# A fused two-block layer on one core: the down-projection weights of each routed expert loaded through GpSimd's software queue

## The chip, the core and the metric
One Trainium2 chip, one core. The engines are TensorE (PE; its weight loads are shown apart as PEld), VectorE (DVE), ScalarE (ACT), GpSimd (POOL) and SyncE (SP). A transfer issued by an engine is carried out by the core's 16 DMA engines; the profile calls SP's queue q1, ACT's q10 and GpSimd's software queue q0. The metric is the device time of one execution in microseconds (us).

## The reference
Two blocks run in series on 512 tokens of width 1024, all in float32. The first mixes by convolutions and spatial gating and looks up single experts (PEER). The second has attention, memory attention and, at its end, the stage of this change, a mixture of 32 experts with four experts for each token:

```python
logits = (hf @ w_router + b_router).astype(jnp.float32)
top_val, top_idx = lax.top_k(logits, TOP_K)          # TOP_K = 4
gates = jax.nn.softmax(top_val, axis=-1)
...
def expert_block(args):
    e, tok, g = args
    xb = hf[tok]
    gu = xb @ w1[e] + b1[e]
    gate = jnp.minimum(gu[:, :D_FF], SWIGLU_LIMIT)
    up = jnp.clip(gu[:, D_FF:], -SWIGLU_LIMIT, SWIGLU_LIMIT)
    act = (up + 1.0) * gate * jax.nn.sigmoid(SWIGLU_ALPHA * gate)
    return (act @ w2[e] + b2[e]) * g[:, None]
```

w1 of an expert is 1024x2048, w2 is 1024x1024; the results are added up for each token, and a last normalisation follows.

## The kernel before
The stages ahead of 2336 us of the span are not touched. The expert stage is one block of code in which each engine runs its own list of instructions and the engines meet at semaphores.

**Weights.** An expert's weights are six chunks of 128 partitions x 4096 floats, 2 MB each: c = 0, 1 gate, 2, 3 up, 4, 5 down-projection. One load is 16 KB for each partition. The SBUF tensor `arena` has nine slots of that size; chunk c of the s-th expert is number i = 6s + c and goes to slot i mod 9 (`placed`). SP issues the 192 loads in this order (L1705 to L1720). Load i waits until load i - 9 has been used: PE counts the semaphore `w_used[c]` up when it is through with a chunk. The first nine have waits of their own, since slots 5 to 8 hold the routing's scratch data: load 5 waits until the routing is done (`slots2` on PE, `gk` on DVE), load 8 until the rows have been written out. From the second expert on the address comes from `expert_at`, which holds the experts ordered by their number of tokens.

**Rows.** GpSimd gathers each expert's rows (64, 96 or 128 of 4 KB, L1743) from HBM into one buffer, `picked`. The gather for expert s waits until PE has transposed the rows of expert s - 1 (`x_t`), and PE waits for it (`rows_in`) in the middle of expert s - 1, behind the up chunks.

**PE, for each expert:** 64 rows at a time, and 32 or 64 more where the expert has 96 or 128 rows. Chunks 0 to 3 in order (`into`, L1803), each behind a wait for its load, with the bias matmuls (L1821) after 1 and 3; then the transposes of the next expert's rows (L1789), the transposes of the activation (L1796), and chunks 4 and 5 (`out_of`, L1815). For wide experts the second part of 4 and 5 comes last, and only then are these slots free. DVE and ACT make the clamped SwiGLU between, and ACT copies and stores the result (L1929, L1934).

**Order of the experts:** the most loaded first by capacity: 96, 96, 128, 64, 128, 64, 128, 64, and then 96 and 64 in turn, 64 last. Behind the 32 experts stand loops for overflow blocks, which have nothing to do for these inputs, and then the block that gathers and adds the results for each token (L2175 to L2218).

Of the kernel before, what the change touches and what calls it, by code (L numbers as in the profile page):

```python
# [40 lines left out]
NE = 32  # L41
# [78 lines left out]
def build(nc, t, out):  # L120
    ctx = ExitStack()
    with ctx:
# [3 lines left out]
        def sem(name):  # L126
            return ctx.enter_context(nc.semaphore(name))
# [30 lines left out]
        pe_done = sem("pe_done")  # L158
        dve_done = sem("dve_done")
# [295 lines left out]
        o = 0  # L455
# [257 lines left out]
        o = 14336  # L713
# [919 lines left out]
        seconds = [sum(len(x) - 1 for x in parts[0:i]) for i in range(NE + 1)]  # L1633

        w_loaded = [sem(f"w_loaded{i}") for i in range(9)]
        w_used = [sem(f"w_used{c}") for c in range(6)]
        rows_out = sem("rows_out")
        rows_in = sem("rows_in")
# [21 lines left out]
        def slot(i):  # L1660
            return arena[:, i * CHUNK:(i + 1) * CHUNK]

        def placed(s, c):
            return (6 * s + c) % 9

        def loads(s, c):
            return 16 * ((6 * s + c) // 9 + 1)

        def after(eng, sem_, count):
            if not isinstance(count, int) or count > 0:  # L1670
# [28 lines left out]
        with nc.Block() as block:  # L1699
            @block.sync  # L1700
            def _(sp):
                sp.dma_start(xn_dram.rearrange("(t p) d -> p t d", p=P), rows[:, :, :]).then_inc(rows_out, 16)
                for s, p in enumerate(ORDER):
                    if s == 0:
                        e6 = 0  # L1705
                    else:
                        if s == 1:
                            sp.wait_ge(dve_done, dv["eati"])
                        e6 = sp.value_load(expert_at[0:1, p:p + 1], min_val=0, max_val=NE - 1) * 6
                    for c in range(6):  # L1710
                        i = 6 * s + c
                        if i == 5:
                            sp.wait_ge(pe_done, pe["slots2"])
                            sp.wait_ge(dve_done, dv["gk"])
                        if i == 8:
                            sp.wait_ge(rows_out, 16)
                        if i >= 9:
                            sp.wait_ge(w_used[(i - 9) % 6], (i - 9) // 6 + 1)
                        src = ew[c, :, :] if s == 0 else ew[bass.ds(e6 + c, 1), :, :].rearrange("o p n -> p (o n)")
                        sp.dma_start(slot(placed(s, c)), src).then_inc(w_loaded[placed(s, c)], 16)  # L1720

                def body(b):
                    e6 = sp.value_load(blk2[0:1, bass.ds(b, 1)], min_val=0, max_val=NE - 1) * 6
                    for c in range(6):
                        sp.wait_ge(w_used[c], b + NE)
                        sp.dma_start(slot(placed(NE, c)), ew[bass.ds(e6 + c, 1), :, :].rearrange("o p n -> p (o n)"))\
                          .then_inc(w_loaded[placed(NE, c)], 16)
                n = each_extra(sp, body)
                for i in range(3):
                    sp.wait_ge(w_loaded[i], 16 * 22)  # L1730
                for c in range(6):
                    sp.wait_ge(w_loaded[placed(NE, c)], n * 16 + loads(NE, c) - 16)
                    sp.sem_inc(all_loaded, 1)

            @block.gpsimd
            def _(eng):
                eng.wait_ge(rows_out, 16)
                eng.wait_ge(dve_done, dv["slots"])
                for s, p in enumerate(ORDER):
                    if s:  # L1740
                        eng.wait_ge(x_t, 2 * s)
                    cap = capacity(p)
                    eng.indirect_dma_start(xg[0:cap, :], None, xn_dram, bass.IndirectOffsetOnAxis(ap=slots[0:cap, p:p + 1], axis=0))\  # L1743
                       .then_inc(rows_in, 16)
                eng.wait_ge(dve_done, dv["slots2"])

                def body(b):
                    eng.wait_ge(x_t, b * 2 + 2 * NE)
                    eng.sem_inc(pool_turn, 1)
                    eng.tensor_copy(curs[:, :], slots2[:, bass.ds(b, 1)]).then_inc(curs_ready, 1)  # L1750
                    eng.wait_ge(curs_ready, b + 1)
                    eng.sem_inc(pool_turn, 1)
                    eng.indirect_dma_start(xg[0:64, :], None, xn_dram, bass.IndirectOffsetOnAxis(ap=curs[:, :], axis=0))\
                       .then_inc(rows_in, 16)
                each_extra(eng, body)

            @block.tensor
            def _(eng):
# [69 lines left out]
                for s, p in enumerate(ORDER):  # L1828
                    w = [slot(placed(s, c)) for c in range(6)]
                    one_hot = hot[:, p:p + 1].to_broadcast([3 * NE, 64])  # L1830
                    nth = [s + 1, seconds[s] + 1]
                    last = len(parts[s]) - 1
                    eng.wait_ge(x_e, 2 * s + 2)
                    for c in range(4):
                        b_, col, done = ((GB, 0, gate_done), (UB, FF, up_done))[c // 2]
                        eng.wait_ge(w_loaded[placed(s, c)], loads(s, c))
                        for i, (r0, nrows) in enumerate(parts[s]):
                            if c == 2 and i == 1:
                                after(eng, y_out[1], seconds[s])
                            mm = into(b_[i], r0, nrows, c, w[c])  # L1840
                            if i == last:
                                mm.then_inc(w_used[c], 1)
                            if c % 2:
                                bias(b_[i], nrows, col, one_hot).then_inc(done[i], 1)
                        if s == 0 and c == 1:
                            eng.wait_ge(dve_done, dv["blkhot2"])
                            for c2 in range(NPAIR):
                                mm = nc.tensor.matmul(bank[0:64, 5, 0:NBO], rowhot2[:, c2, :], blkhot2[:, c2, :],
                                                      start=c2 == 0, stop=c2 == NPAIR - 1)
                            mm.then_inc(pe_done, 1)  # L1850
                    if s + 1 < NE:
                        eng.wait_ge(rows_in, 16 * (s + 2))
                        transpose_rows(capacity(ORDER[s + 1]), 0)
                    if s == 0:
                        eng.wait_ge(dve_done, dv["slots2"])
                    eng.wait_ge(act_ok[0], nth[0])
                    transpose_act(0, 64)
                    if s + 1 < NE:
                        transpose_rows(capacity(ORDER[s + 1]), 1)
                    eng.wait_ge(h_e[0], nth[0])  # L1860
                    after(eng, y_out[0], s)
                    eng.wait_ge(w_loaded[placed(s, 4)], loads(s, 4))
                    mm = out_of(0, 64, 4, w[4])
                    if last == 0:
                        mm.then_inc(w_used[4], 1)
                    else:
                        eng.wait_ge(act_ok[1], nth[1])
                        transpose_act(1, parts[s][1][1])
                    eng.wait_ge(w_loaded[placed(s, 5)], loads(s, 5))
                    mm = out_of(0, 64, 5, w[5])  # L1870
                    if last == 0:
                        mm.then_inc(w_used[5], 1)
                    bias(YB[0], 64, 2 * FF, one_hot).then_inc(y_done[0], 1)
                    if last:
                        nrows = parts[s][1][1]
                        eng.wait_ge(h_e[1], nth[1])
                        for c in range(4, 6):
                            out_of(1, nrows, c, w[c]).then_inc(w_used[c], 1)
                        bias(YB[1], nrows, 2 * FF, one_hot).then_inc(y_done[1], 1)
# [3 lines left out]
                def body(b):  # L1883
# [4 lines left out]
                    eng.wait_ge(x_e, b * 2 + 2 * (NE + 1))  # L1888
                    for c in range(4):
                        b_, col, done = ((GB, 0, gate_done), (UB, FF, up_done))[c // 2]  # L1890
                        eng.wait_ge(w_loaded[placed(NE, c)], b * 16 + loads(NE, c))
                        into(b_[0], 0, 64, c, wx[c]).then_inc(w_used[c], 1)
                        if c % 2:
                            eng.wait_ge(hot2_ready, b + 1)
                            bias(b_[0], 64, col, hot2).then_inc(done[0], 1)
# [2 lines left out]
                    eng.wait_ge(h_e[0], b + (NE + 1))  # L1898
                    eng.wait_ge(y_out[0], b + NE)
                    for c in range(4, 6):  # L1900
                        eng.wait_ge(w_loaded[placed(NE, c)], b * 16 + loads(NE, c))
                        out_of(0, 64, c, wx[c]).then_inc(w_used[c], 1)
                    bias(YB[0], 64, 2 * FF, hot2).then_inc(y_done[0], 1)
                each_extra(eng, body)
# [365 lines left out]
```

## Time and profile before

| | us |
|---|---|
| median of 3 runs | 3464.08 |
| lowest and highest | 3462.27, 3466.59 |
| the profiled execution | 3457.53 |
| its span | 3455.6 |
| expert stage, from its first load's issue to PE's last matmul | 2336.7 to 3412.8 |

PE is busy 82% of the span, DVE 39%, ACT and POOL 18% each; the granted clock of PE is 0.959 over the whole. In the slices of the page the DMA engines are at nine tenths or more from the sixth slice to the nineteenth, where expert rows of the first block are gathered, and again from the twenty-eighth to the thirty-ninth, the stage of this change; PE is there at nine tenths too. So an average doesn't tell which of the two sets the pace: one has to cut the stage into stretches and to look for gaps of either. A queue's share of 16 engines is the time of its packets over the time of the stretch; a packet's time includes waiting beside another that is in flight, so sums somewhat over 100% are full engines.

### The profile page before, as it was taken

The numbers are of one execution on the slowest core, as the hardware profiler recorded it, in microseconds if no ns is written. First come the engines' busy times: TensorE is split into PE (matmuls) and PEld (weight loads), VectorE is DVE, ScalarE is ACT, GpSimd is POOL, SyncE is SP. The second block draws the span as 40 slices with busy tenths as digits, with TensorE's granted clock in tenths as the row PEclk, the third lists the DMA queues.
The fourth block names the chain that finished last, engine by engine and source line by source line (L and its number), as shares of the span: only waits on it lengthen the run. The fifth ranks groups of instructions, "written<-read, shape, count | busy, mean of one in ns | idle before, by whom it ended". The sixth has DMA issues, their size and how long they took to land. (4 is left out here: it accounts for less than half of the span.)

```text
span 3455.6 us, 30126 instructions
## 1 busy us (share of the span) xinstructions
PE 2841.8 (82%) x11525; PEld 1202.6 (35%) x11525; DVE 1360.9 (39%) x2703; ACT 635.3 (18%) x1774; POOL 636.1 (18%) x609
## 2 busy tenths in 40 slices
PE   6989377777777777777689889986999999999894
PEld 3435232222222222222344445542333333333331
DVE  1933666756766676544420441134111111111113
ACT  1110022222222222222230431110000000000001
POOL 0200143443343344343200200020000000000002
PEclk9989699999999999999999899997999999999997
DMA  4210199999999999999821602107999999999997
GB/s 153 98 67 1 72 421 422 421 421 421 421 419 421 415 419 416 422 417 422 362 79 58 207 13 98 49 22 307 423 399 389 406 408 410 414 408 404 411 408 294
DMA packets 152801, 1057.01 MB, mean 306 GB/s; under 512 B 16240, under 2 KB 20848, under 8 KB 62320
## 3 DMA queue, kind: packets, MB, share of 16 engines
q0 software_dynamic: 79232, 556.31, 39.1%
q1 hardware_dynamic: 65136, 487.75, 35.5%
q10 hardware_dynamic: 8288, 11.02, 0.9%
q8 instruction: 91, 1.49, 0.2%
q14 instruction: 54, 0.44, 0.0%
HBM read 1025.66 MB, written 29.36 MB: 305 GB/s over the span
## 5 line engine op out<-in xcount | busy, mean ns | idle before, releaser
L986 PE MATMUL banks<-arena,aT 128*128 128x512 f32 x2048 | 962.1, 614 | 374.1 <-ACT aT L972 372.6
L946 DVE SCALAR_TENSOR_TENSOR arena<-arena 128x1024 f32<-128x1024 f32 x512 | 627.3, 1225 | 493.3 <-DMA arena<-in_expert_uv,picked 489.3
L986 PEld LDWEIGHTS banks<-arena,aT 128*128 128x128 f32 x2048 | 375.2, 193 | 960.3 <-ACT aT L972 573.1
L926 POOL DMA_INDIRECT arena<-in_expert_uv,picked x512 | 513.7, 1003 | 1014.2 <-PE banks L986 745.6
L1803 PE MATMUL banks<-arena,aT 128*64 128x512 f32 (+1 forms) x4032 | 607.5, 501 | 15.3 <-DMA arena<-in_expert_w 14.6
L1803 PEld LDWEIGHTS banks<-arena,aT 128*64 128x64 f32 (+1 forms) x4032 | 208.4, 125 | 388.6 <-issue 340.3
L1815 PE MATMUL banks<-arena,aT 128*64 128x512 f32 (+1 forms) x2016 | 311.8, 510 | 9.0 <-ACT aT L1924 8.9
L2118 DVE TENSOR_SCALAR aT<-banks 128x512 f32<-128x512 f32 (+1 forms) x49 | 30.2, 615 | 632.7 <-PE banks L1821 632.7
L962 ACT ACTIVATE aT<-aT 128x2 f32<-128x2 f32 x256 | 52.1, 203 | 938.4 <-DVE arena L946 938.4
L1743 POOL DMA_INDIRECT picked<-ffn_rows,slots x32 | 30.5, 954 | 1003.4 <-PE banks L1789 949.4
L383 PE MATMUL banks<-arena 128*128 128x512 f32 x384 | 172.5, 610 | 20.5 <-PEq L529 12.1
L972 ACT ACTIVATE aT<-cst,aT 128x128 f32<-128x128 f32 x512 | 173.6, 386 | 0.0
L1815 PEld LDWEIGHTS banks<-arena,aT 128*64 128x64 f32 (+1 forms) x2016 | 105.6, 127 | 181.8 <-issue 149.7
L238 PE MATMUL banks<-aT,arena 128*128 128x512 f32 x320 | 140.0, 599 | 1.0 <-PEq L1034 1.0
L2125 DVE TENSOR_SCALAR aT<-banks 128x512 f32<-128x512 f32 (+1 forms) x49 | 30.1, 613 | 262.7 <-PE banks L1821 262.7
L966 ACT ACTIVATE aT<-aT,picked 128x1 f32<-128x1 f32 x512 | 122.8, 286 | 8.4
L747 PE MATMUL banks<-aT,arena 128*128 128x512 f32 x256 | 113.9, 599 | 1.2 <-PEq L361 1.2
L383 PEld LDWEIGHTS banks<-arena 128*128 128x128 f32 x384 | 74.7, 197 | 114.9 <-issue 114.9
L646 PE MATMUL banks<-aT,arena 128*128 128x512 f32 x240 | 103.4, 592 | 1.0 <-PEq L282 1.0
L1924 ACT ACTIVATE aT<-banks 128x512 f32<-128x512 f32 (+1 forms) x49 | 26.3, 536 | 405.3 <-PE banks L1796 405.3
L238 PEld LDWEIGHTS banks<-aT,arena 128*128 128x128 f32 x320 | 61.5, 193 | 78.8 <-issue 78.8
L1919 ACT ACTIVATE aT<-aT 128x512 f32<-128x512 f32 (+1 forms) x49 | 27.9, 569 | 307.9 <-DVE aT L2118 307.9
(301 smaller groups left out, 1986.5 us busy)
## 6 DMA issues: line engine op xcount, KB each, us to landing
arena<-in_expert_w SPq DMA_DIRECT2D x192, 2048.0 KB, 29.9
arena<-in_w_in SPq DMA_DIRECT2D x7, 2048.0 KB, 12.9
expert_rows<-aT ACTq DMA_DIRECT2D x70, 128.0 KB, 8.9
arena<-in_w_out SPq DMA_DIRECT2D x4, 2048.0 KB, 7.8
arena<-in_w_q SPq DMA_DIRECT2D x4, 2048.0 KB, 8.0
arena<-in_expert_uv,picked POOLq DMA_INDIRECT x512
arena<-in_w_mem_kv SPq DMA_DIRECT2D x4, 2048.0 KB, 8.1
expert_rows<-h SPq DMA_DIRECT2D x4, 2048.0 KB, 18.2
```

What stands on the lines that cost most here:

```text
L238: mm = nc.tensor.matmul(dst(j % 8), lhsT, rhs, start=start, stop=stop)
L383: mm = nc.tensor.matmul(bank[:, (2 * tt + n) % 4, :], src[:, k, tt * P:(tt + 1) * P], chunk_view(c0 + n)[:, k, :], start=k == 0, stop=k == ...
L646: mm = nc.tensor.matmul(bank[:, j % 8, :], w[:, k, col:col + P], aT[:, k, :], start=k == 0, stop=k == KD - 1)
L747: mm = nc.tensor.matmul(bank[:, g % 4, :], w[:, k, g % 4 * P:(g % 4 + 1) * P], aT[:, k, :], start=k == 0, stop=k == KD - 1)
L926: eng.indirect_dma_start(slot[n % RING], None, uv_rows, bass.IndirectOffsetOnAxis(ap=eidx[:, n:n + 1], axis=0))\
L946: nc.vector.scalar_tensor_tensor(out=u, in0=u, scalar=1.0, in1=tok[:, tt, :], op0=ALU.mult, op1=ALU.mult, accum_out=dots[:, k:k + 1]).then ...
L962: nc.scalar.activation(gelus[:, k:k + PAIR], dots[:, k:k + PAIR], ACT.Gelu_apprx_tanh)\
L966: nc.scalar.activation(acts[:, k + i:k + i + 1], gelus[:, k + i:k + i + 1], ACT.Copy, scale=gates[:, n + i:n + i + 1]).then_inc(acts_done, 1)
L972: nc.scalar.activation(diag[:, (n + i) % RING, :], ident, ACT.Copy, scale=acts[:, k + i:k + i + 1]).then_inc(diag_done, 1)
L986: mm = nc.tensor.matmul(bank[:, 2 * (tt % 2) + half, :], diag[:, n % RING, :], slot[n % RING][:, D + half * NC:D + (half + 1) * NC], start ...
L1803: mm = nc.tensor.matmul(bank[tile, b_, 0:width], xT[:, c % 2 * 4 + k, r0:r0 + nrows], w[:, k * D + lo:k * D + lo + width], start=c % 2 == ...
L1815: mm = nc.tensor.matmul(bank[tile, YB[i], 0:width], hv[:, kk % nj, kk // nj * nrows:(kk // nj + 1) * nrows], w[:, k * D + lo:k * D + lo + ...
```

## The change
Chunks 4 and 5 of each expert are issued by GpSimd, through its software queue, on semaphores of their own (`w_loaded_soft`). SP keeps chunks 0 to 3. GpSimd's list becomes, for each expert: gather the rows, read the expert's number, load chunk 4, load chunk 5, each with the same `w_used` wait that SP had for it. Slots, sizes and addresses are the same, and PE's wait for a load now names the semaphore of the queue that brings it. SP's wait for the routing, which stood ahead of load 5, stands ahead of load 6 (chunk 0 of the second expert), and GpSimd has the same one ahead of its load 5. GpSimd's load 4 stands behind the first gather.

```diff
+        w_loaded_soft = [sem(f"w_loaded_soft{i}") for i in range(9)]
...
         def loads(s, c):
-            return 16 * ((6 * s + c) // 9 + 1)
+
+            by_pool = 4 <= c and s < NE
+            same = sum(1 for x in range(6 * s + c + 1) if x % 9 == placed(s, c) and (4 <= x % 6 and x // 6 < NE) == by_pool)
+            return (w_loaded_soft if by_pool else w_loaded)[placed(s, c)], 16 * same
...
-                    for c in range(6):
+                    for c in range(4):
                         i = 6 * s + c
-                        if i == 5:
+                        if i == 6:
                             sp.wait_ge(pe_done, pe["slots2"])
                             sp.wait_ge(dve_done, dv["gk"])
...
+                for i in range(9):
+                    sp.wait_ge(w_loaded_soft[i], 16 * sum(1 for x in range(6 * NE) if x % 9 == i and 4 <= x % 6))
...
+                    e6 = eng.value_load(expert_at[0:1, p:p + 1], min_val=0, max_val=NE - 1) * 6 if s else 0
+                    for c in range(4, 6):
+                        i = 6 * s + c
+                        if i == 5:
+                            eng.wait_ge(pe_done, pe["slots2"])
+                            eng.wait_ge(dve_done, dv["gk"])
+                        if i >= 9:
+                            eng.wait_ge(w_used[(i - 9) % 6], (i - 9) // 6 + 1)
+                        src = ew[c, :, :] if s == 0 else ew[bass.ds(e6 + c, 1), :, :].rearrange("o p n -> p (o n)")
+                        eng.dma_start(slot(placed(s, c)), src).then_inc(w_loaded_soft[placed(s, c)], 16)
...
-                        eng.wait_ge(w_loaded[placed(s, c)], loads(s, c))
+                        eng.wait_ge(*loads(s, c))
```

How this stands on the engines at the start of the stage. On GpSimd before, from the stage's first instruction: the gathers (`picked`) of the first five experts, one behind the other.

```order
60 L1743 DMA picked<-ffn_rows,slots 96x1024 [waits dve_done,rows_out]
61 L1743 DMA picked<-ffn_rows,slots 96x1024 [waits x_t]
62 L1743 DMA picked<-ffn_rows,slots 128x1024 [waits x_t]
63 L1743 DMA picked<-ffn_rows,slots 64x1024 [waits x_t]
64 L1743 DMA picked<-ffn_rows,slots 128x1024 [waits x_t]
```

The same place with the change: gathers L1749, loads of chunks 4 and 5 L1760 (`arena`), reading the expert's number L1751.

```order
60 L1749 DMA picked<-ffn_rows,slots 96x1024 [waits dve_done,rows_out]
61 L1760 DMA arena<-in_expert_w 128x4096
62 L1760 DMA arena<-in_expert_w 128x4096 [waits dve_done,pe_done]
63 L1749 DMA picked<-ffn_rows,slots 96x1024 [waits x_t]
64 L1751 TENSOR_LOAD expert_at
65 L1751 ISA x2
66 L1760 ISA [waits w_used1]
67 L1760 DMA arena<-in_expert_w 128x4096
68 L1760 ISA [waits w_used2]
69 L1760 DMA arena<-in_expert_w 128x4096
70 L1749 DMA picked<-ffn_rows,slots 128x1024 [waits x_t]
```

The second gather, which followed the first directly, now stands behind the first expert's chunk 5 and behind the wait for the routing; each later gather stands behind two loads.

On SP before, at the same place: five loads of the first expert, the sixth behind the routing's wait, then those of the second expert.

```order
63 L1702 DMA ffn_rows<-arena 128x4x1024
64 L1720 DMA arena<-in_expert_w 128x4096 x5
65 L1720 DMA arena<-in_expert_w 128x4096 [waits dve_done,pe_done]
66 L1709 TENSOR_LOAD expert_at [waits dve_done]
67 L1709 ISA x2
68 L1720 ISA
69 L1720 DMA arena<-in_expert_w 128x4096
70 L1720 ISA
71 L1720 DMA arena<-in_expert_w 128x4096
```

On SP with the change:

```order
63 L1706 DMA ffn_rows<-arena 128x4x1024
64 L1724 DMA arena<-in_expert_w 128x4096 x4
65 L1713 TENSOR_LOAD expert_at [waits dve_done]
66 L1713 ISA x2
67 L1724 ISA [waits dve_done,pe_done]
68 L1724 DMA arena<-in_expert_w 128x4096
69 L1724 ISA
70 L1724 DMA arena<-in_expert_w 128x4096
```

The routing's wait now stands ahead of chunk 0 of the second expert, so that this load and GpSimd's chunk 5 are released together.

## Rows read from the trace of the kernel before

**Rows 1.** The page: busy time, a group of PE, the loads from issue to landing
```profile
PE 2841.8 (82%) x11525; PEld 1202.6 (35%) x11525; DVE 1360.9 (39%) x2703; ACT 635.3 (18%) x1774; POOL 636.1 (18%) x609
...
L1803 PE MATMUL banks<-arena,aT 128*64 128x512 f32 (+1 forms) x4032 | 607.5, 501 | 15.3 <-DMA arena<-in_expert_w 14.6
...
arena<-in_expert_w SPq DMA_DIRECT2D x192, 2048.0 KB, 29.9
```

**Rows 2.** Stretches: length, busy us of each engine, granted clock, DMA share, GB/s
```profile
2370.00:2387.00 17.00, 15.29 (x130) 6.67 (x132) 3.78 (x10) 2.82 (x4) 0.92 (x1) 0.82 0.09 26
...
2624.00:2630.00 6.00, 6.00 (x32) 1.98 (x28) 0.00 (x0) 0.60 (x1) 0.00 (x0) 1.00 0.43 98
2630.00:3397.00 767.00, 724.98 (x5268) 276.00 (x5266) 96.07 (x169) 67.55 (x134) 20.88 (x23) 0.98 1.01 409
```

**Rows 3.** DMA issues in 2386:2387, in 2400:2628, in 2628.5:2629.5: median us to landing
```profile
arena<-in_expert_w SPq DMA_DIRECT2D x1, 2048.0 KB, 7.8
...
arena<-in_expert_w SPq DMA_DIRECT2D x36, 2048.0 KB, 18.1
...
arena<-in_expert_w SPq DMA_DIRECT2D x1, 2048.0 KB, 7.7
```

**Rows 4.** Waits of PE and of SP's queue, 2420 to 3420: us, times, longest
```profile
PE banks L1803 <- DMA arena<-in_expert_w: 14.6, 12, 2.3
...
SPq L1720 <- PE banks L1803: 504.9, 118, 7.6
```

**Rows 5.** Timeline at the first experts; then landing of gathers issued in 2372:2374 and 2399:2400
```profile
2372.95 0.92 POOL L1743 DMA_INDIRECT picked<-ffn_rows,slots  x1 [9.32 <-PE banks L1789]
...
2397.53 0.55 PE L1789 MATMUL banks<-cst,picked 96*128 96x96 f32 x4
...
2399.27 0.20 PEld L1815 LDWEIGHTS banks<-arena,aT 128*64 128x64 f32 x4 [0.54 <-ACT aT L1924]
...
2427.40 0.20 PEld L1803 LDWEIGHTS banks<-arena,aT 128*64 128x64 f32 x4 [0.41 <-issue]
...
2433.18 0.65 PE L1789 MATMUL banks<-cst,picked 128*128 128x128 f32 x4
...
picked<-ffn_rows,slots POOLq DMA_INDIRECT x1, 4.0
...
picked<-ffn_rows,slots POOLq DMA_INDIRECT x1, 12.2
```

**Rows 6.** DMA in 2481:2487, 3315:3320, 3208:3214, 1600:1690: total, then packets, MB, share
```profile
DMA packets 275, 2.56 MB, mean 427 GB/s; under 512 B 25, under 2 KB 25, under 8 KB 150
q1 hardware_dynamic: 141, 2.05, 80.5%
q0 software_dynamic: 134, 0.51, 21.1%
...
DMA packets 171, 1.63 MB, mean 325 GB/s; under 512 B 8, under 2 KB 8, under 8 KB 93
q1 hardware_dynamic: 86, 1.28, 81.3%
q0 software_dynamic: 85, 0.35, 21.7%
...
DMA packets 173, 2.57 MB, mean 429 GB/s; under 512 B 16, under 2 KB 16, under 8 KB 16
...
DMA packets 5205, 37.92 MB, mean 421 GB/s; under 512 B 577, under 2 KB 577, under 8 KB 577
```

**Rows 7.** The last load (issued in 3368:3369) and PE in the last expert, timeline
```profile
arena<-in_expert_w SPq DMA_DIRECT2D x1, 2048.0 KB, 39.3
...
3368.48 0.33 SPq L1720 DMA_DIRECT2D arena<-in_expert_w  x1
...
3398.04 0.20 PEld L1803 LDWEIGHTS banks<-arena,aT 128*64 128x64 f32 x4 [1.01 <-DMA arena<-in_expert_w]
...
3405.49 7.09 PE L1815 MATMUL banks<-arena,aT 128*64 128x512 f32 x32 [0.69 <-ACT aT L1924]
```

More of the change, by code:

```diff
@@ L1728, in _ @@
                 n = each_extra(sp, body)
+                for i in range(9):
+                    sp.wait_ge(w_loaded_soft[i], 16 * sum(1 for x in range(6 * NE) if x % 9 == i and 4 <= x % 6))
                 for i in range(3):
-                    sp.wait_ge(w_loaded[i], 16 * 22)
+                    sp.wait_ge(w_loaded[i], 16 * sum(1 for x in range(6 * NE) if x % 9 == i and x % 6 < 4))
                 for c in range(6):
-                    sp.wait_ge(w_loaded[placed(NE, c)], n * 16 + loads(NE, c) - 16)
+                    sp.wait_ge(w_loaded[placed(NE, c)], n * 16 + (loads(NE, c)[1] - 16))
                     sp.sem_inc(all_loaded, 1)
@@ L1861, in _ @@
                     after(eng, y_out[0], s)
-                    eng.wait_ge(w_loaded[placed(s, 4)], loads(s, 4))
+                    eng.wait_ge(*loads(s, 4))
                     mm = out_of(0, 64, 4, w[4])
@@ L1868, in _ @@
                         transpose_act(1, parts[s][1][1])
-                    eng.wait_ge(w_loaded[placed(s, 5)], loads(s, 5))
+                    eng.wait_ge(*loads(s, 5))
                     mm = out_of(0, 64, 5, w[5])
@@ L1890, in body @@
                         b_, col, done = ((GB, 0, gate_done), (UB, FF, up_done))[c // 2]
-                        eng.wait_ge(w_loaded[placed(NE, c)], b * 16 + loads(NE, c))
+                        eng.wait_ge(w_loaded[placed(NE, c)], b * 16 + loads(NE, c)[1])
                         into(b_[0], 0, 64, c, wx[c]).then_inc(w_used[c], 1)
@@ L1900, in body @@
                     for c in range(4, 6):
-                        eng.wait_ge(w_loaded[placed(NE, c)], b * 16 + loads(NE, c))
+                        eng.wait_ge(w_loaded[placed(NE, c)], b * 16 + loads(NE, c)[1])
                         out_of(0, 64, c, wx[c]).then_inc(w_used[c], 1)
```

## The prediction
> **What bounds the kernel now.** I read the page first, then the stretches, then the waits. On the page [rows 1] TensorE (PE) is busy 82% of the span, but the matmuls of this change (L1803 and, for the down-projection, L1815) lie in one stage, from about 2337 us on. The 192 expert loads of 2048 KB all leave from SyncE, by the hardware queue q1; GpSimd's software queue q0 carries row gathers only there. Cut into stretches [rows 2], the stage shows two regimes. Up to 2630 us the DMA engines have gaps (share 0.09 in 2370:2387, 0.43 in 2624:2630) while PE is busy without a break: early, PE sets the pace, because the experts with 96 and 128 rows come first and the ring of nine slots is full. From 2630 to 3397 us the DMA share is 1.01 at 409 GB/s and PE has 42 us of 767 free: there the DMA sets the pace. The last gap ends when a load goes out at 2628.5:2629.5 and lands 7.7 us later [rows 3], an idle queue's figure. After it nothing is idle until the last load, issued at 3368.5 and landing 39.3 us later, at 3407.8 [rows 7]. So the path is: PE from expert 0 until it frees that slot, then bytes, then whatever PE has left once the last load is in.
>
> Two consequences. A PE stall before 2628 us moves the end one for one; one after it costs nothing while loads are queued (PE already waits 12 times for a load there, 14.6 us in all [rows 4]). And it matters which load is the last to land.
>
> **The change, part by part.** Removed from SP: 64 loads; added to GpSimd: 64 loads, 31 register loads and the waits. A GpSimd gather takes 0.92 us to issue [rows 5]; taking a load for the same, two loads and a gather cost it about 3 us in an expert's 31. GpSimd is otherwise waiting there (9.3 us before its second gather [rows 5]): nothing. SP's issues waited for PE's slots (504.9 us on L1803 alone [rows 4]), so its lighter queue gains nothing either. c4 of expert 0 now leaves behind the first gather, at about 2364 instead of 2341 us; it lands near 2371, in front of a DMA gap that lasts until 2387 [rows 2], and PE wants it at 2399.27 [rows 5]. Nothing; without that gap it would cost 5 us.
>
> *How the two queues share.* The trace has q0 and q1 together only at gathers. In 2481:2487, a 128-row gather, they sent 134 and 141 packets, together 427 GB/s; q1 alone made 429, and q0 alone, with the 8 KB rows of the earlier stage, 421 [rows 6]. So an engine takes a row of one queue and a row of the other in turn, and the sum of the rates holds. In 3315:3320, a 96-row gather, the turns are the same (85 and 86) but the rate is 325. The software loads have 128 partitions, as the first gather has, so I take 427. Their own rows are 16 KB, which q0 never carries here: the bound upward is q0's 421 against 429, 64 loads of 4.9 us times 1.9%, 6 us; the bound below is no change. I take no change, since the 128-row case is nearest, and keep 6 us for the range.
>
> The Trainium skill, DMA: Bandwidth & Descriptors, section Latency and other measured facts, says DMA engines 7 and 15 are usually slower, by its best guess because the software queue's descriptor rings contend for their ports. It speaks against this change; by it the sum would be 3489 instead of 3483 us. The 421 beside 429 leans its way, but the row sizes differ too.
>
> *Expert 0, the first term.* In program order GpSimd now does: c5 of expert 0 (behind the same slots2 wait as SP's, released at 2386.5), then the gather for expert 1, then c4 and c5 of expert 1. Before, that gather left at 2372.95 and landed in 4.0 us [rows 5], long before PE's transposes at 2397.53. Now it stands in q0 behind a 2 MB load. What a transfer takes beside its data is 2.9 us where the queue was empty (a 2 MB load landed 7.8 us after its issue [rows 3], 4.9 of them data at 427 GB/s), and some 6 us where it was full (128 rows landed in 12.2 us [rows 5], 6.1 of them turns of 20 KB at 427). c5 leaves at 2386.5 plus one GpSimd issue, 2387.6, into a queue that just fills: 2.9. Its 8 rows on each engine take turns with SP's: 4.19 MB, 9.8 us. Behind it the gather's 96 rows of 4 KB alternate with 96 of 16 KB: 1.97 MB at 325 GB/s, 6.0 us. It lands at 2387.6 + 2.9 + 9.8 + 6.0 = 2406.3, and PE stands from 2397.5 to then: **9 us**, bounds 7 (the gather at 427) and 12 (the full queue's 6 us). The output matmuls could not have started before 2399.27 [rows 5], but what they waited for also stands behind these transposes in PE's order, so nothing is hidden. PE is the pace there, so all 9 us arrive at 2628. A pause may also lower the granted clock; the rows show 0.82 in 2370:2387 behind the idle start [rows 2]; that is inside the upper bound.
>
> Later gathers don't stall. The one for expert s+2 is issued in the middle of expert s, behind c5 of s+1, and needed in the middle of s+1, some 30 us on. In front of it stand at most two loads at half rate, 20 us, and its own 6.
>
> *Loads c0 to c3 come later in each expert.* With q0 busy, q1 has half the rate: c2 and c3 lose up to two load times, 10 us. Tightest is c3 of expert 1. Ahead of it or beside it go c5 of expert 0, the gather and the other five loads of expert 1: with c3 itself 15.1 MB, 36 us at 421 GB/s, so it lands near 2426. PE used it from 2427.40 before [rows 5], and would 9 us later now: 2436. From there to 2628 us a load leaves when the one nine places back is used up, so PE wants it eight loads on, some 45 us at the 5.8 us that it took for c3 of expert 1 (2427.40 to 2433.18 [rows 5]); the 36 loads of that time landed after 18.1 us (median, [rows 3]), and 10 more still leaves 17. Nothing. After 2630 us PE will stand a few us at c3 of many experts, then find c4 and c5 in place. That costs nothing, as the queues stay filled: c0 to c3 of the next expert are issued by then.
>
> *The tail, the second term.* Bytes are the same, so the last landing moves by the 9 us alone: 3416.8. But the last to land is no more c5 of expert 31. q0 took its two loads at half rate from the middle of expert 30 on; q1 ends alone, with c3. Before, PE started c3 at 3398.04 and the output matmuls at 3405.49 [rows 7], 7.45 us with bias, activation and transposes, and c4 and c5 took 7.09 us, to 3412.6. They had hidden beside the transfer of c4 and c5. Now PE has all that left: 3416.8 + 0.2 + 7.45 + 7.09 = 3431.5, which is **19 us** over 3412.6: 9 from the start and 10 from the tail. If c2 also lands with it, 3.5 us more; if q0's last load is the later, 3.5 to 10 less. Behind it, store, final gathers and adds are as before, in series.
>
> Sum: the profiled execution took 3457.5 us (span 3455.6), with the change 3476.5. Against the median of 3464.1, 6.6 us above that one, it is **3483 us**.
>
> **Rivals.**
> *No loss.* The two rings keep each engine fuller than one. To pay back 19 us over the 767 us of the DMA regime, the rate must go from 409 to 419 GB/s or more; it decides from there, and gives 3464 at 419, and under 3457 from 423. For: 409 includes the slow 96-row gathers, and 421 to 429 is seen. Against: 427 with both queues beside 429 with one. The Trainium skill, same page, section Issuing engines are not separate DMA queues, says that issuing from several engines only saves sequencer time; by that alone the time stays at 3464. The trace agrees on the shared engines, but the rule doesn't look at order. 18% for this rival.
> *Rows split.* GpSimd might cut 16 KB rows to 4 KB. Turns of 20 KB on 16 engines take 0.77 us at 427 GB/s and give q0 a fifth of the bytes: c5 of expert 0 needs 32 of them, 25 us instead of 10, and each expert's gather waits behind 50. 15 us more at least: 3498, and 3540 if PE stands 1.3 us an expert besides. 8%.
> *Slow turns.* The software loads meet whatever slows the 96-row gathers, and go at 325 GB/s beside q1. Two thirds of an expert's bytes (8.4 MB) then take 25.8 instead of 19.6 us: 31 times 6.2, 190 us: 3675. 5%.
> *It doesn't do what it says*: the order of instructions shows that it does.
>
> **How the numbers follow.** Forecast 69%: 3483, by its own bounds 3474 (7 at the start, nothing of the tail) to 3496 (12, 6 of rate, 3.5 more of tail). The range 3466 to 3504 reaches a good way into the no-loss rival and takes the small end of split rows; it leaves out the rest, under 20%. Within 0.2% is within 7 us, about what a measurement tells: of the no-loss 18%, 6 are faster and 12 the same, and 4 of the forecast's edge are the same: faster 6%, same 16%, slower 78%.
>
> **What the profile will show.** Right: q0 with about 134 MB more; PE standing some 9 us at the row transposes of L1789 from 2397.5 on behind a gather of picked; the last DMA gap ending near 2638; a mean near 409 GB/s behind it; c4 and c5 of expert 31 landing 10 us before c3, PE's last output matmul at 3431. Wrong: a mean over 415 or under 400 GB/s, packets of 4 KB in q0, no stall at 2398, or last landing by q0.

## The result, and the profile after

The changed kernel takes 3476.8 us (median of 6 runs, 3475.6 to 3479.5); the kernel before took 3463.2 us in the runs beside it. The ratio is 1.0040, with a 95% interval of 1.0027 to 1.0053: slower by 9 to 18 us, 14 at the middle. The profiled execution took 3477.2 us, its span is 3475.5 us. That is 19.9 us over the span of before, but 1.7 of them were there when the expert stage began (2338.0 instead of 2336.3 us), in code that did not change, and the executions of one kernel differ by some us (the profiled one of before, 3457.5 us, is among its fastest). So I compare sections of the stage, and medians for verdicts.

The page of the changed kernel shows the loads divided, and what each queue's loads took from issue to landing:

```profile
q0 software_dynamic: 88448, 690.53, 47.9%
q1 hardware_dynamic: 55920, 353.53, 26.1%
...
L1760 POOL DMA_DIRECT2D arena<-in_expert_w x64 | 34.4, 537 | 739.4 <-PE banks L1819 716.3
...
arena<-in_expert_w SPq DMA_DIRECT2D x128, 2048.0 KB, 32.5
arena<-in_expert_w POOLq DMA_DIRECT2D x64, 2048.0 KB, 15.4
```

q0 has 134 MB more than before, q1 134 MB less. GpSimd issues a load in 0.54 us. A load in q0 lands 15.4 us after its issue, one in q1 32.5 (29.9 before, [rows 1]): the software queue is the short one, since it gets its turns beside a long one.

PE's waits in the stage, 2400 to 3440 us (us in total, times, longest), which answer to [rows 4]:

```profile
PE banks L1812 <- DVE aT L2146: 26.6, 15, 2.2
PE banks L1819 <- DMA arena<-in_expert_w: 21.6, 18, 3.9
PE banks L1805 <- DMA picked<-ffn_rows,slots: 10.0, 1, 10.0
```

Two waits have grown: one of 10.0 us for a row gather, which did not exist in this stretch, and those for loads, from 14.6 to 21.6 us. The timeline of the changed kernel at expert 0, against [rows 5]:

```profile
2388.61 0.54 POOL L1760 DMA_DIRECT2D arena<-in_expert_w  x1 [22.93 <-DVE slots L2157]
2389.45 0.97 POOL L1749 DMA_INDIRECT picked<-ffn_rows,slots  x1 [0.30 <-issue]
...
2409.38 0.90 PE L1805 MATMUL banks<-cst,picked 96*128 96x96 f32 x4 [9.96 <-DMA picked<-ffn_rows,slots]
...
2411.82 4.22 PE L1831 MATMUL banks<-arena,aT 128*64 128x512 f32 x16
```

GpSimd issues chunk 5 when the routing is done, then the gather for expert 1, and PE gets its rows at 2409.4. The load itself, by the DMA issues of 2388:2389 in the changed kernel, landed 14.8 us after its issue, the one that SP issued beside it 10.0:

```profile
arena<-in_expert_w SPq DMA_DIRECT2D x1, 2048.0 KB, 10.0
arena<-in_expert_w POOLq DMA_DIRECT2D x1, 2048.0 KB, 14.8
```

And the stretch behind the early regime, 2650:3380, before and then changed (columns as in [rows 2]):

```profile
2650.00:3380.00 730.00, 689.78 (x5044) 262.65 (x5046) 92.15 (x163) 63.96 (x128) 20.88 (x23) 0.98 1.01 409
```
```profile
2650.00:3380.00 730.00, 681.04 (x4974) 258.86 (x4970) 91.72 (x161) 63.83 (x127) 47.08 (x70) 0.99 1.01 412
```

The DMA engines are as full as before and move slightly more (412 against 409 GB/s), and yet PE has done 9 us less work in the same time (e3 below, which has no stall at expert 0, shows the same: 683.1 us at 412 GB/s). So the software queue costs no bandwidth. What is left is the order in which the loads arrive, and what PE's clock did; the experiments below take these up.

For all kernels I read two sections from PE's timeline. **A** runs from the stage's first matmul to the first down-projection matmul of expert 0, so it holds the gather's wait; **B** from there to the last bias matmul of expert 31. The before kernel: A 62.9, B 1013.5 us (for instance 2399.27 [rows 5] to the end of the bias matmul that starts at 3412.41). The changed kernel: A 73.8, B 1019.6 us. So the change cost 10.9 us in A and 6.1 in B, together 17 between these two executions; the run behind the stage, 42 to 44 us in every kernel, is not touched. The medians are only 14 us apart, so if A holds its 10.9, about 3 us are left for the second term by the medians, where the two profiles say 6.1.

Not all of B's 6.1 us are waits. The last output group took 8.79 us where before it took 7.09 [rows 7]; the granted clock was 0.81 in 3422.45:3431.24 and 1.00 in the same group before. That alone is 1.7 us.

### The profile page after: what moved, and what is told of

Its sections match the earlier page's. It is cut to its first block and busy times, and to the rows that moved or that the text cites. A ratio compares the mean times of both kernels' runs of the same rounds, so it can differ in the third digit from the quotient of the medians.

```text
span 3475.5 us, 30229 instructions
## 1 busy us (share of the span) xinstructions
PE 2845.1 (82%) x11525; PEld 1204.5 (35%) x11525; DVE 1361.8 (39%) x2703; ACT 635.1 (18%) x1774; POOL 675.0 (19%) x673
## 2 busy tenths in 40 slices
DMA packets 152803, 1057.03 MB, mean 304 GB/s; under 512 B 16240, under 2 KB 20848, under 8 KB 62320
## 3 DMA queue, kind: packets, MB, share of 16 engines
q0 software_dynamic: 88448, 690.53, 47.9%
## 5 line engine op out<-in xcount | busy, mean ns | idle before, releaser
L1819 PE MATMUL banks<-arena,aT 128*64 128x512 f32 (+1 forms) x4032 | 611.9, 503 | 25.5 <-DMA arena<-in_expert_w 21.6
L1760 POOL DMA_DIRECT2D arena<-in_expert_w x64 | 34.4, 537 | 739.4 <-PE banks L1819 716.3
L1749 POOL DMA_INDIRECT picked<-ffn_rows,slots x32 | 31.9, 997 | 269.1 <-PE banks L1805 216.1
## 6 DMA issues: line engine op xcount, KB each, us to landing
arena<-in_expert_w SPq DMA_DIRECT2D x128, 2048.0 KB, 32.5
arena<-in_expert_w POOLq DMA_DIRECT2D x64, 2048.0 KB, 15.4
arena<-in_w_in SPq DMA_DIRECT2D x7, 2048.0 KB, 12.8
```

Of the source, the lines that this page charges most:

```text
L1819: mm = nc.tensor.matmul(bank[tile, b_, 0:width], xT[:, c % 2 * 4 + k, r0:r0 + nrows], w[:, k * D + lo:k * D + lo + width], start=c % 2 == ...
```

## The experiments

Theory before them, as in the prediction: 9 (now 10) us of stall at expert 0, passed on in full, and a tail because chunk 3, no more chunk 5, lands last. Rivals: the software queue is slower for its bytes (A); only the first stall counts (B); such a stall is mostly caught up later (C).

| kernel | ratio to before | 95% interval | A, us | B, us |
|---|---|---|---|---|
| before | 1 | | 62.9 | 1013.5 |
| changed | 1.0040 | 1.0027 to 1.0053 | 73.8 | 1019.6 |
| e1: last expert's loads by SP | 1.0036 | 1.0024 to 1.0048 | 73.4 | 1019.8 |
| e2: gather ahead of chunk 5 | 1.0006 | 0.9997 to 1.0015 | 62.6 | 1019.0 |
| e3: both | 1.0009 | 1.0000 to 1.0018 | 62.6 | 1020.3 |
| e4: before, with a late gather | 1.0039 | 1.0026 to 1.0053 | 77.5 | 1013.6 |
| e5: before, last expert in another order | 1.0027 | 1.0019 to 1.0036 | 64.6 | 1027.4 |
| e6: before, 128-row gathers | 0.9947 | 0.9933 to 0.9960 | 62.6 | 998.7 |
| e7: e3 with 128-row gathers | 0.9967 | 0.9955 to 0.9978 | 62.6 | 1009.0 |
| e8: as e7, first 24 experts only | 0.9955 | 0.9941 to 0.9968 | 62.6 | 1002.0 |
| e9: as e7, chunk 5 only, of all 32 experts | 0.9954 | 0.9940 to 0.9967 | 62.6 | 1000.0 |
| e10: as e7, chunks 3 to 5, of all 32 experts | 1.0016 | 1.0007 to 1.0025 | 62.6 | 1024.0 |
| e11: e2, first 24 experts only | 0.9984 | 0.9975 to 0.9993 | 62.6 | 1013.5 |

**The first term alone (e2, and e4 from the other side).** In e2 the gather for expert 1 goes back in front of chunk 5 and its wait:

```diff
+                def gather(s):
...
                         if i == 5:
+                            gather(1)
                             eng.wait_ge(pe_done, pe["slots2"])
```

> The changed kernel with the gather of the second expert's rows moved ahead of the wait for the routing and of chunk 5 of the first expert, where it stood before; nothing else. Theory: PE's wait of 10.0 us for that gather goes, the last DMA gap ends some 11 us earlier, and all of it arrives at the end: 3465 to 3468. Rival A (slower queue): no change. Rival C (a stall there is largely caught up later, since the last landing moved by only 5 to 7 us): 5 us or less, 3472 or more.

Measured 3463.7 us against 3460.7 for before and 3476.8 for the changed kernel: the wait is gone, A is 62.6 again, and some 12 us went with it (from 1.0040 to 1.0006). Nothing of the stall had been caught up. But what is left over before is 3 us, with an interval from -1 to 5. e4 puts a stall of the same kind into the kernel before, without any software load:

```diff
                     if s:
                         eng.wait_ge(x_t, 2 * s)
+                    if s == 1:
+                        eng.wait_ge(w_used[3], 1)
```

> The kernel before, with one more wait: the gather of the second expert's rows waits until PE has used chunk 3 of the first expert, so that PE stands about 10 to 12 us for it. No software loads. Theory (PE is the pace until 2628 us, bytes behind): all of it arrives, 3473 to 3475. Rival C (caught up later): 3468 or less.

Its waits of PE for gathers over the whole stage, the first expert's included:

```profile
PE banks L1791 <- DMA picked<-ffn_rows,slots: 23.9, 2, 13.1
```

The new wait is 13.1 us, A grew by 14.6, B not at all (1013.6), and the time by 15 us, 3475.7 against 3460.7. So a PE stall at expert 0 arrives in full at the end, and rival C falls. Rival A falls with e2: 64 loads by the software queue and a loss of 3 us, 5 at most. Rival B, that only the first stall counts, is not touched by either; by the times alone e2 agrees with it.

**The second term (e1, e3, e5).** e1 gives chunks 4 and 5 of the last expert back to SP, behind chunk 3:

```diff
-            by_pool = 4 <= c and s < NE
+            by_pool = 4 <= c and s < NE - 1
...
-                    for c in range(4):
+                    for c in range(6 if s == NE - 1 else 4):
```

> The changed kernel with the last expert's chunks 4 and 5 issued by SyncE again, in the old order; the other 31 experts as changed. Theory (a stall at expert 0 and a tail at expert 31): the last load to land is chunk 5 again, PE's work between last landing and last matmul falls from 16.8 us to about 5, and the time falls by 10 to 12 us, to 3465 to 3467. Rival A (the software queue is slower for its bytes): no change, 3477. Rival B (only the stall at expert 0 counts): no change, 3477.

Measured 3475.3 us; B is 1019.8, where the theory wanted 1009. A miss: what both rivals wanted. (By the intervals the edit may have gained some us, up to about 7, but not the 10 to 12.) e3, with both edits:

> Both of the edits: gather of the second expert ahead of chunk 5, and the last expert's chunks by SyncE. Theory: both terms go, 13.6 us at least, so 3463 or less; if the rate of 410 to 412 GB/s that the changed kernel showed behind its last DMA gap, against 407 to 409 before, is the two queues' doing, another 5 to 6 us: 3456 to 3458, faster than the kernel before. Rival A (software queue slower): stays above 3470.

Measured 3465.5 against 3460.7: A as before, B still 1020.3. Another miss, and neither term of rate nor tail came; against e2 (1.0009 and 1.0006) the last expert's order gained nothing. What PE did in the last expert of e1:

```profile
3351.68 3.65 PE L1821 MATMUL banks<-arena,aT 128*64 128x512 f32 x16 [0.70 <-DMA arena<-in_expert_w]
...
3403.55 7.09 PE L1821 MATMUL banks<-arena,aT 128*64 128x512 f32 x32
...
3410.69 7.04 PE L1821 MATMUL banks<-arena,aT 128*64 128x512 f32 x32
...
3421.52 8.58 PE L1833 MATMUL banks<-arena,aT 128*64 128x512 f32 x32 [0.69 <-ACT aT L1942]
```

From 3352 us on PE waits 0.7 us for loads in all, and comes to chunk 0 of expert 31 only at 3403.6, against 3387.2 before. 11.2 us of that are the later start of its B, and some 5 are new. The last load (issue in 3380:3390, landing 29.7 us later) is in at 3414.6, when PE is still at chunks 2 and 3:

```profile
arena<-in_expert_w SPq DMA_DIRECT2D x1, 2048.0 KB, 29.7
```

So which load came last didn't matter any more: PE itself was late, with loads lying ready that it had not come to. Was the tail's mechanism wrong in itself? e5 takes the kernel before, all loads by SP, and changes only the order in the last expert:

```diff
-                    for c in range(6):
+                    for c in ((4, 5, 0, 1, 2, 3) if s == NE - 1 else range(6)):
```

> The kernel before, all loads by SyncE, with the last expert's chunks loaded in the order 4, 5, 0, 1, 2, 3. No software loads, no stall at expert 0. Theory (the order of landing in the last expert is worth 10 us): chunk 3 lands last, 10 to 12 us of PE's work move behind it, 3473 to 3475. Rival A (slower software queue is what cost): 3463.

Measured 3470.5 against 3461.2, 2.5 us under the range that was expected, though clearly over the rival's 3463; B 1027.4. There PE does wait for the last loads, and reaches the output matmuls 12 us later than before (3405.49 in [rows 7]):

```profile
3409.98 3.65 PE L1803 MATMUL banks<-arena,aT 128*64 128x512 f32 x16 [1.20 <-DMA arena<-in_expert_w]
...
3417.69 9.79 PE L1815 MATMUL banks<-arena,aT 128*64 128x512 f32 x32 [0.69 <-ACT aT L1924]
```

Its chunks 0 to 2 were also issued later, since SP stood at chunk 4's wait, and its last output group ran 2.7 us longer (9.79 against 7.09, at a granted clock of 0.72 in 3417.69:3427.48), so not all of it need be the landing order. The last load landed at 3409.9 here (issue 3373.3, 36.6 us) and PE's last matmul ended 17.8 us behind it, against 5.0 before: 12.8 more, 10.1 without the slower clock. The mechanism exists and has about the size forecast, in a kernel whose PE keeps up with its loads. The changed kernel's PE does not.

**A version with more room (e6), and the new theory (e7 to e11).** The trace of before had shown 325 GB/s in a shared stretch with a 96-row gather and 427 with a 128-row one [rows 6]. e6 is the kernel before with one line changed, so that each gather fetches 128 rows, the surplus unused:

```diff
-                    cap = capacity(p)
+                    cap = P
```

> The kernel before, with every row gather of 128 rows instead of 64, 96 or 128; the surplus rows are not used. More bytes (1.2 MB in 8 to 9 MB of gathers), but a 128-row gather kept 427 GB/s beside q1 and a 96-row one only 325. Theory (partition count slows the mixed stretch, and the DMA regime's length is what counts): each narrower gather lost about 1 to 1.5 us of queue time, some 24 of them lie in the DMA regime: 20 to 35 us gained there at most, less what PE then limits (it has 42 us free there, so it should not bind fully); 3440 to 3450. Rival (a gather of 4 KB rows costs by its rows): 4 to 10 us slower, 3467 to 3473.

Measured 3442.8 against 3461.2, as the theory wanted, 18 us faster than the kernel before, with more bytes: 5.8 MB by the pages (q0 562.07 against 556.31 MB), not the 1.2 MB of the expectation. The shared stretch 3301.5:3307.5 of e6, first, then 3100:3300 of the kernel before (queues as in [rows 6]):

```profile
DMA packets 278, 2.55 MB, mean 425 GB/s; under 512 B 28, under 2 KB 28, under 8 KB 154
q1 hardware_dynamic: 140, 2.03, 80.0%
q0 software_dynamic: 138, 0.52, 21.5%
```
```profile
DMA packets 7447, 81.63 MB, mean 408 GB/s; under 512 B 1072, under 2 KB 1456, under 8 KB 2704
```

and 3100:3300 of e6, which moves 427 GB/s where before moved 408:

```profile
DMA packets 7908, 85.34 MB, mean 427 GB/s; under 512 B 1090, under 2 KB 1474, under 8 KB 3010
```

PE has no wait for a load left in e6; it is the pace from end to end. Its B is 14.8 us shorter than before's, and before's waits for loads were 14.6 [rows 4]: that was all that faster loads could give. That makes e6 the better base to see what the software queue's loads cost:

> The changed kernel with the gather of the second expert ahead of chunk 5, the last expert's chunks by SyncE, and every gather of 128 rows. Theory: the sum of the single edits, so 5 us or so under the kernel before with 128-row gathers: 3435 to 3448. Rival (the two queues gain nothing in rate): equal to the kernel before with 128-row gathers.

e7 took 3449.4, 6.6 us over e6 and outside both expectations, and PE waits for loads again, which it did not with the same bytes in e6:

```profile
PE banks L1826 <- DMA arena<-in_expert_w: 7.8, 9, 2.3
```

This is new theory P: while the software queue has loads, SP's queue gets every second turn, its chunks 0 to 3 come late while 4 and 5 come early, PE stands for the late ones late in the stage, and the time lost there can't be won back in the few experts that are left. e8 lets the last 8 experts run in the old order:

```diff
-            by_pool = 4 <= c and s < NE
+            by_pool = 4 <= c and s < 24
```

> 128-row gathers, the second expert's gather ahead of chunk 5, and chunks 4 and 5 by GpSimd for the first 24 experts only; SyncE loads all six chunks of the last 8. New theory (P): PE's own chain is the path; the software queue makes chunks 0 to 3 land late, PE stands for them at wide experts late in the stage, and cannot catch up in the one or two experts that are left. With 8 experts in the old order PE has caught up: PE's waits for loads fall from 7.8 us to under 2, and the time is that of the kernel before with 128-row gathers, 3441 to 3445. Rival (a cost for each software load, wherever): three quarters of the 6.6 us stay, 3447 to 3448.

Measured 3445.3, B 1002.0, with one wait of 1.3 us; between the two expectations by its median (3441 to 3445 and 3447 to 3448), and its interval covers both. e9 has chunk 5 alone in the software queue:

> 128-row gathers, the second expert's gather ahead of chunk 5, and only chunk 5 of each expert by GpSimd (32 loads instead of 64). Theory P: chunks of SyncE's queue are late by at most one load time instead of two; PE's waits for loads fall to 0 to 3 us, 3442 to 3446. Rival (a cost for each software load): half of 6.6 us, 3446; told apart by PE's waits in the trace.

3444.2, B 1000.0, waits for loads 2.0 us: as P wants, though 3446 lies within its interval. The same on the base of the kernel before is clearer:

> Gathers as in both kernels (64, 96, 128 rows), the second expert's gather ahead of chunk 5, chunks 4 and 5 by GpSimd for the first 24 experts only. Theory P: PE's waits and the end are those of the kernel before, 3459 to 3462; if the 410 to 412 GB/s in the shared stretch count, since bytes are the limit again in the last experts, 2 to 4 us less. Rival: 3464 to 3465, as with all 32 experts.

3455.8 against 3461.7, faster than before by 2 to 9 us, and B is 1013.5, as before, not 1019 to 1020. A cost for each software load is refuted by it, for 48 of the 64 loads still go by the software queue, and so is rival B: between e2 and e11 only the last 8 experts' loads differ, and the ratios are 1.0006 and 0.9984.

That doesn't mean that the time is lost in these 8 experts. PE's first matmuls of expert 24 and of expert 31, in the kernel before, the changed one and e11:

```profile
3155.75 2.80 PE L1803 MATMUL banks<-arena,aT 128*64 128x512 f32 x12 [2.16 <-DMA arena<-in_expert_w]
...
3387.17 7.09 PE L1803 MATMUL banks<-arena,aT 128*64 128x512 f32 x32
```
```profile
3173.73 2.75 PE L1819 MATMUL banks<-arena,aT 128*64 128x512 f32 x12
...
3404.48 7.09 PE L1819 MATMUL banks<-arena,aT 128*64 128x512 f32 x32
```
```profile
3162.94 2.32 PE L1826 MATMUL banks<-arena,aT 128*64 128x512 f32 x10
...
3385.38 2.79 PE L1826 MATMUL banks<-arena,aT 128*64 128x512 f32 x12
```

Counted from the start of B (2399.27, 2411.82 and 2399.24 us), the changed kernel is 5.4 us behind before at expert 24 and 4.8 at expert 31; e11 is 7.2 behind at expert 24 and 1.8 ahead at expert 31. The lag is older than the last 8 experts in both. With SP's old order e11 wins it back there; with software loads the changed kernel keeps it, and so does e2 (3.7 behind, then 2.8), which differs from e11 in these experts' loads alone.

What the lag consists of is less clear. PE's waits for loads fit P in the changed kernel (21.6 us against 14.6) and in e3 (19.0), but e1 has 16.0 and e2 15.0. In e2's profile it is the clock that fell: 0.97 granted in 3140:3400, where before had 0.99 (0.02 of 260 us is 5 us), and 0.71 in its last output group, 9.97 us instead of 7.09. No run separates the two, and over all its executions e2's granted clock is that of before, 0.958.

e10 goes the other way, chunks 3, 4 and 5:

> 128-row gathers, the second expert's gather ahead of chunk 5, and chunks 3, 4 and 5 by GpSimd (96 loads instead of 64). Theory P: the two queues share each expert half and half all the time, so that chunks 0 to 2 are later than before by up to three load times and chunk 3 is no later; PE's waits at chunks 1 and 2 grow, to 8 to 20 us in all, 3450 to 3462. Rival (a cost for each software load): 1.5 times 6.6 us, 3452 to 3453, without new waits of PE for loads.

3467.7, B 1024.0. The size is a little over the upper end of P, and the place is another:

```profile
PE banks L1810 <- DMA picked<-ffn_rows,slots: 32.7, 10, 6.3
```

No wait for loads in the stage at all, but PE stands for the row gathers, which now have three loads ahead of them in their queue. So P named the wrong victim there: with three software loads it is the gather that is late, not chunks 1 and 2.

## Why the prediction was right, and where it was not

The change made the kernel slower by 14 us where 19 were forecast, within the range, for one reason that held and one that was put in the wrong place. That PE's last output matmul ended at 3431.2 in the profile, where 3431 was forecast, is in part luck: 1.7 us were there before the stage, and the second term came from elsewhere.

*What bounds the kernel.* Held: PE until about 2630 us, bytes behind it. e4 passed its stall on in full, and e6 shows from the other side that the later regime hung on the bytes. What the forecast missed is how near the two are. It read PE's "42 us free of 767" as room. By PE's waits in 2630:3397 of the kernel before, only a third of it is waiting for loads; the rest is PE's own chain through DVE and ACT:

```profile
PE banks L1796 <- DVE aT L2130: 21.1, 12, 1.8
PE banks L1803 <- DMA arena<-in_expert_w: 14.6, 12, 2.3
PE banks L1815 <- ACT aT L1924: 6.2, 20, 0.4
```

So PE had 14.6 us to spare, 2%, and a lag of a few us near the end takes several experts to win back. So the no-loss rival could have paid back 14.6 us at most, not the 19 it needed: at a higher rate PE sets the pace, as in e6.

*Expert 0, 9 us with bounds 7 to 12.* The wait measured 10.0 us and the section 10.9. Behind the wait PE ran slower: the row transposes at 2409.38 took 0.90 us where they had taken 0.55 [rows 5], and the first output group, which counts in B, 4.22 us instead of 3.65; the granted clock in 2400:2430 was 0.83 where it had been 1.00. The steps: chunk 5 landed 14.8 us after its issue, where 12.7 were reckoned, at 2403.4; the gather's rows were there 6 us behind it, as reckoned. The last DMA gap ended with a load issued between 2641 and 2642 us, where 2638 was forecast.

*Later gathers don't stall.* Held for two loads ahead of a gather: 10.0 us for one gather is all there is. e10 shows the margin: with three loads, 32.7 us in ten waits, spread over the stage.

*Turns and rate, no change taken, bounds 0 to 6 us slower.* The turns held: in 3355:3365 of the changed kernel q0 sent 145 packets and q1 147, at 431 GB/s together. At expert 0 the two loads issued together took 14.8 and 10.0 us all the same: in 2391:2394 q0 had sent 16 packets when q1 had sent 61, and only from then on did they go evenly (59 and 57 in 2394:2398). The forecast gave both the same start. The rate came out 412 against 409 GB/s in 2650:3380, 0.7% more, outside the bounds on the fast side. The part of the no-loss rival that rested on a higher rate was real but far smaller than it needed, and PE's lag ate it. Only e11, where PE keeps up at the end, shows something for it, 0.16% less time than before; that the rate is its cause was not shown by a run of its own. By the guess on two slow DMA engines in the Trainium skill (DMA: Bandwidth & Descriptors, section Latency and other measured facts) the changed kernel should have been slower in bytes; the total rate here gives no sign of it, and the rate of single engines was not looked at.

*The tail, 10 us: the step that failed.* The landings came as forecast: chunk 3 of expert 31 was the last, at 3414.8 us (3416.8 forecast), 10.3 us behind chunk 5. But PE was not waiting for it:

```profile
3373.20 0.33 SPq L1724 DMA_DIRECT2D arena<-in_expert_w  x1
...
arena<-in_expert_w SPq DMA_DIRECT2D x1, 2048.0 KB, 41.6
...
3411.62 7.04 PE L1819 MATMUL banks<-arena,aT 128*64 128x512 f32 x32
...
3422.45 8.79 PE L1831 MATMUL banks<-arena,aT 128*64 128x512 f32 x32 [0.69 <-ACT aT L1940]
```

It ran through chunks 2 and 3 without a pause and came to chunk 3 half way, near 3415.1, by its own lateness. Two paths ended within half a us of each other, the forecast saw one, and taking that one away brings nothing while the other stands. The second term measured 6.1 us between the profiles and about 3 by the medians, and e1 and e3, which take away the landing order of expert 31 that the sum rested on, took no measurable part of it away. The prediction said of PE's pauses at chunk 3 behind 2630 us that they cost nothing, as the queues stay filled. That is true of the bytes and not of PE: each pause leaves PE with loads lying ready, and from 3352 us on (in e1) it works without a break and is itself the path. e11 shows that the last 8 experts decide whether PE's lag is won back. How much of the lag is late loads and how much the clock stays open.

*The lower bound.* "3474 (7 at the start, nothing of the tail)" doesn't add up: 3464 and 7 are 3471. The measured 3476.8 is inside with either.

*The split of rows and the slow turns* did not occur: 8192 packets more in q0 is 64 loads of 128 rows (q0 had 79232 before and 88448 after; the other 1024 are 16 for each load, and the page's count of packets under 512 B is the same, 16240), so rows stay whole, and the rate did not fall.

## What to carry to other kernels

A second queue doesn't only share the work, it changes the order in which transfers arrive: here the short queue's loads landed 15.4 us after their issue and the long one's 32.5, and a small transfer behind a big one in the same queue waits for it. Before a load goes to a queue, look at what else in that queue somebody waits for, and issue that first. When you read how much room an engine has, count only its waits for the resource in question, not all its idle time. And where two resources run within a few per cent of each other, a pause of the one that is not the pace is free only as long as enough of the run is left to win it back; look at the last stretch separately.

## What the runs showed of the hardware

Beside a full queue of 16 KB rows on 128 partitions, a gather of 96 rows runs the shared stretch at 325 GB/s [rows 6] and one of 128 rows at 425 to 427; making all gathers of the stage 128 rows, at 85.3 instead of 81.6 MB moved in 200 us, gave 0.53% (0.40 to 0.67) of the whole time and the fastest kernel here, 3442.8 us. Why the narrower gather slows the other queue was not tried further. A transfer of 2 MB by the software queue moved at the hardware queue's rate (431 GB/s for both in 3355:3365 of the changed kernel), in turns of one row each, by the packet counts (145 and 147 there; 134 and 141 with rows of 4 and 16 KB [rows 6]), and took GpSimd 0.54 us to issue, less than a gather's 0.92.
